# The RMS norms between the stages of a two-layer transformer trunk: squares summed by TensorE in four token parts, root and reciprocal on a quarter of the columns

## What is computed

```python
def rmsnorm(x, g):
    xf = x.astype(jnp.float32)
    y = xf * lax.rsqrt(jnp.mean(xf * xf, axis=-1, keepdims=True) + EPS)
    return (y * g.astype(jnp.float32)).astype(x.dtype)
...
def ffn_sublayer(s, m, i, g, wg, wu, wd):
    h = modulate(rmsnorm(s, g), m[3 * i], m[3 * i + 1])
    return s + 0.5 * m[3 * i + 2] * swiglu(h, wg, wu, wd)
...
    x = ffn_sublayer(x, mx, 0, p['g_ffn1'], p['w1g'], p['w1u'], p['w1d'])
    h = modulate(rmsnorm(x, p['g_mix']), mx[3], mx[4])
    u = h @ p['w_in']
    ...
    x = x + mx[5] * y
    x = ffn_sublayer(x, mx, 2, p['g_ffn2'], p['w2g'], p['w2u'], p['w2d'])
```

## Time and profile before

| | |
|---|---|
| median of 3 runs | 2639.79 us (2638.39 to 2639.95) |
| the profiled execution's own time | 2638.57 us |
| its span, first to last instruction | 2636.7 us |
| mean granted TensorE clock | 0.994 of full speed |
| TensorE matmul busy | 2554.9 us, 97% |
| VectorE, ScalarE, GpSimd busy | 2069.8, 1012.5, 163.7 us |

### The profile page before, as it was taken

One profiled execution on the slowest core, in us unless ns is written; L12 is line 12 of the kernel. 1 busy time (PEld: TensorE's weight loads), 2 busy tenths in 40 slices (PEclk: granted clock), 3 DMA queues, 4 the chain that ended last, 5 costly groups with the idle time before them and its releaser, 6 DMA issues. The chain is left out here.

```text
span 2636.7 us, 42699 instructions
## 1 busy us (share of the span) xinstructions
PE 2554.9 (97%) x15356; PEld 2363.0 (90%) x15356; DVE 2069.8 (79%) x3414; ACT 1012.5 (38%) x1854; POOL 163.7 (6%) x314
## 2 busy tenths in 40 slices
PE   6999999999997999999999899999998998999999
PEld 5899999988965889999999799999997866989998
DVE  5688888887958388888888888777768956688885
ACT  4333433333147333422332433234324256344443
POOL 2000000020003200000000200000002003100001
PEclk8999999999999999999999999999999999999999
DMA  8234323332111113333334123343232201223332
GB/s 295 64 120 136 116 92 114 124 104 64 55 57 49 33 56 105 117 93 115 123 103 136 48 90 119 98 130 119 91 104 72 88 24 47 79 83 109 99 101 79
DMA packets 192361, 253.97 MB, mean 96 GB/s; under 512 B 7278, under 2 KB 130268, under 8 KB 192220
## 3 DMA queue, kind: packets, MB, share of 16 engines
q1 hardware_dynamic: 192220, 252.07, 30.4%
HBM read 249.95 MB, written 2.10 MB: 96 GB/s over the span
## 5 line engine op out<-in xcount | busy, mean ns | idle before, releaser
L1211 PE MATMUL ps<-h_hi,w_hi 128*128 128x384 f32 (+2 forms) x2368 | 790.5, 334 | 21.9 <-DVE h_lo L2326 18.2
L1213 PE MATMUL ps<-h_hi,w_lo 128*128 128x384 f32 (+2 forms) x2368 | 785.3, 332 | 0.0
L1212 PE MATMUL ps<-h_lo,w_hi 128*128 128x384 f32 (+2 forms) x2256 | 749.3, 332 | 0.0
L1211 PEld LDWEIGHTS ps<-h_hi,w_hi 128*128 128x128 f32 x2368 | 449.3, 190 | 53.6 <-issue 22.5
L1213 PEld LDWEIGHTS ps<-h_hi,w_lo 128*128 128x128 f32 x2368 | 449.3, 190 | 20.7
L1212 PEld LDWEIGHTS ps<-h_lo,w_hi 128*128 128x128 f32 x2256 | 428.0, 190 | 19.2 <-issue 1.0
L1811 ACT ACTIVATE w_hi<-raw 128x512 fp32r<-128x512 f32 x464 | 279.7, 626 | 420.8 <-PE ps L1213 327.8
L2468 DVE TENSOR_TENSOR w_lo<-raw,w_hi 128x512 fp32r<-128x512 f32 x464 | 307.5, 684 | 14.8 <-ACT w_hi L1811 14.8
L1211 PE MATMUL ps<-t_hi_all,w_hi 128*128 128x384 f32 x864 | 292.1, 338 | 0.0
L1213 PE MATMUL ps<-t_hi_all,w_lo 128*128 128x384 f32 x864 | 292.0, 338 | 0.0
L1212 PE MATMUL ps<-t_lo_all,w_hi 128*128 128x384 f32 x864 | 291.9, 338 | 0.0
(11 more groups left out here) (276 smaller groups left out, 3994.1 us busy)
## 6 DMA issues: line engine op xcount, KB each, us to landing
side_raw<-in_w_ada SPq DMA_DIRECT2D x240, 256.0 KB, 2.7
raw<-in_w_ffn_gate SPq DMA_DIRECT2D x44, 1024.0 KB, 5.4
raw<-in_w_ffn_up SPq DMA_DIRECT2D x44, 1024.0 KB, 5.4
raw<-in_w_ffn_down SPq DMA_DIRECT2D x44, 1024.0 KB, 5.0
raw<-in_w_in SPq DMA_DIRECT2D x14, 1024.0 KB, 5.3
ada_buf<-in_w_ada SPq DMA_DIRECT2D x12, 1024.0 KB, 12.4
raw<-in_w_out SPq DMA_DIRECT2D x8, 1024.0 KB, 5.7
raw<-in_w_in SPq DMA_DIRECT2D x8, 512.0 KB, 7.2
```

Of the source, the lines that this page charges most:

```text
L1211: mm(out, wh, xh, start=start, stop=False, skip_group_check=reopened)
L1212: mm(out, wh, xl, start=False, stop=False, skip_group_check=reopened)
L1213: return mm(out, wl, xh, start=False, stop=stop, skip_group_check=reopened)
```

## The change

GpSimd's additions are gone for q = 1 to 5. Instead ScalarE writes the squares into a ring of four blocks, `sq4`, and TensorE sums them itself (`sum_squares`): each block j is four fp32 matmuls with 32 columns of ones as weights, one for each quarter of the segment's tokens, into partitions 0-31, 32-63, 64-95 and 96-127 of one bank. After the eight blocks the bank holds the sums of 64 token columns (context) or 128 (latent), a different quarter of the tokens on each group of 32 partitions. Root and reciprocal work on these 64 or 128 columns. Then TensorE spreads the result (`spread`): four fp32 matmuls with one column of the identity matrix, repeated 128 times, as weights write `rstd` of all tokens on all partitions into another bank, and VectorE's `tn` reads it from there. The plan keeps the bank of the sums out of the round from `open` to `close`, and the bank of a spread until `unblock`; the next user of the latter waits for `t_done` of the norm's last block.

The order changes with it: the sums are put between the down-projection's groups, the mixer's output groups and the blocks of the next stage's first pass; ScalarE's and VectorE's split of the second weight tile of the next stage moves behind the first root and reciprocal. The core of the diff:

```diff
+    def open(self, q, s):
+        bank = self.next_bank()
+        self.slots[("stat", q, s)] = (None, bank, self.uses[bank])
+        self.uses[bank] += 1
+        self.blocked.add(bank)
+        if bank in self.held:
+            self.spread_before[("stat", q, s)] = self.held.pop(bank)
...
+    def close(self, q, s):
+        _, bank, use = self.slots[("stat", q, s)]
+        self.slots[("stat", q, s)] = (self.n, bank, use)
+        self.n += 1
+        self.blocked.remove(bank)
...
+    def spread(self, q, s):
+        self.slot(("spread", q, s))
+        bank = self.slots[("spread", q, s)][1]
+        self.uses[bank] -= 1
+        self.blocked.add(bank)
+    def unblock(self, q, s):
+        bank = self.slots[("spread", q, s)][1]
+        self.blocked.remove(bank)
+        self.held[bank] = (q, s)
...
+        if f:
+            self.unblock((0, 2, 3, 5)[f], second)
...
+                if s == second and after < 3 * DEPTH:
+                    a_, b_ = seg_order(after)
+                    if j == 0:
+                        self.open(after, a_)
+                    if j == 1:
+                        self.close(after, a_)
+                    if j == 3:
+                        self.spread(after, a_)
+                        self.open(after, b_)
...
-        for s in (1, 0):
-            for h in range(HEADS):
-                self.slot(("K", l, h, s))
+        q = 3 * l + 1
+        keys = [("K", l, h, 1) for h in range(HEADS)]
+        for key in keys:
+            self.slot(key)
+        self.close(q, 0)
+        self.spread(q, 0)
+        self.renumber(keys)
+        self.unblock(q, 1)
+        for h in range(HEADS):
+            self.slot(("K", l, h, 0))
+            if h % 2:
+                pass
+        self.unblock(q, 0)
...
+            def sum_squares(q, s, js):
+                o, n = PIECES[s][:2]
+                bank = bank_of(("stat", q, s))
+                for j in js:
+                    if j == 0:
+                        wait_bank(pe, ("stat", q, s))
+                    pe.wait_ge(sq_done, sqcount(q, s, j))
+                    for c in range(4):
+                        at_ = n // 4 * c
+                        last = mm(ps[32 * c:32 * c + 32, bank, 0:n // 4], ones[:, 0:32], square_of(q, s, j)[:, at_:at_ + n // 4],
+                                  start=(j == 0), stop=(j == KD - 1), skip_group_check=True)
+                    if j < 4:
+                        last.then_inc(sq_summed, 1)
+                    elif j == KD - 1:
+                        last.then_inc(products, 1)
+            def spread(q, s):
+                n = PIECES[s][1] // 4
+                wait_bank(pe, ("spread", q, s))
+                pe.wait_ge(rstd_ready, rstd_number(q, s))
+                for c in range(4):
+                    last = mm(ps[:, bank_of(("spread", q, s)), n * c:n * c + n], ident[:, 32 * c:32 * c + 1].to_broadcast([128, 128]),
+                              fourths(q, s, rstd4), start=True, stop=True, skip_group_check=True)
+                last.then_inc(products, 1)
...
+                                if s == first and ws == SUM_PASS[f]:
+                                    sum_squares(q, second, sums_first(ws, k, f))
+                                    if k == SPREAD_AT[f]:
+                                        spread(q, second)
...
+                        if s == second and after < 3 * DEPTH:
+                            a_, b_ = seg_order(after)
+                            if j < 2:
+                                sum_squares(after, a_, range(4 * j, 4 * j + 4))
+                            if j == 3:
+                                spread(after, a_)
+                            if j >= 3:
+                                sum_squares(after, b_, (j - 3,))
...
+                        if s == 1 and k < 3:
+                            sum_squares(q, 0, (5 + k,))
                         if s == 1 and k == 4:
-                            stat(q, 0)
+                            spread(q, 0)
...
+                        first, second = seg_order(q + 1)
+                        if slots[0][0] == ("out", l, 4, first):
+                            sum_squares(q + 1, first, range(4))
+                            sum_squares(q + 1, second, range(4))
+                        if slots[0][0] in (("out", l, 6, first), ("out", l, 7, first)):
+                            sum_squares(q + 1, first, (slots[0][0][2] - 2,))
+                        if slots[0][0] == ("out", l, 4, second):
+                            sum_squares(q + 1, first, (6, 7))
+                        if slots[0][0] == ("out", l, 5, second):
+                            spread(q + 1, first)
+                        if slots[0][0] in (("out", l, 6, second), ("out", l, 7, second)):
+                            sum_squares(q + 1, second, (slots[0][0][2] - 2,))
...
+                if between(q):
+                    if j >= 4:
+                        act.wait_ge(sq_summed, summed_number(q, s, j - 4))
...
-                if nxt:
-                    split(nxt[1])
-                for j in range(2):
-                    square(q, second, j)
...
+                square(q, second, 0)
                 root(q, first)
+                split(nxt[1])
+                square(q, second, 1)
                 square(q, second, 2)
...
+                    if between(q) and j == 0:
+                        wait_products(dve, ("spread", q, s))
                     stt(out=tn[:, j % 2, o:o + n], in0=xT[:, j, o:o + n], scalar=amul[:, q // 3, q % 3, j, v:v + 1],
-                        in1=rstd[:, o:o + n], op0=ALU.mult, op1=ALU.mult).then_inc(t_done, 1)
+                        in1=pt(("spread", q, s), n) if between(q) else rstd[:, o:o + n], op0=ALU.mult, op1=ALU.mult)\
+                        .then_inc(t_done, 1)
...
-                    split(nxt[1])
-                    add_one(2, second)
                     last_seg = second
                     first, second = seg_order(q)
                     over_rms(q, first)
+                    add_one(2, last_seg)
+                    split(nxt[1])
```

More of the change, by code:

```diff
@@ L96, with between, sums_first @@
 SUM_NUMBER = {5: 1, 6: 2, 7: 3, 3: 4}
+def between(q):
+    return 0 < q < 3 * DEPTH
+def sums_first(w, k, f):
+    want = {"gu": {0: (5,), 1: (6,), 2: (7,)}, "g": {1: (6,), 3: (7,)}}[SUM_PASS[f]]
+    return want.get(k, ()) if w == SUM_PASS[f] else ()
 def segs_of(norm):
@@ L216, in __init__ @@
         self.bank = 0
+        self.blocked = set()
+        self.held = {}
+        self.spread_before = {}
         self.uses = [0] * 8
@@ L260, in hold, with compact @@
         self.chunk += n
+    def compact(self):
+        order = sorted((x[0], key) for key, x in self.slots.items())
+        for n, (_, key) in enumerate(order):
+            self.slots[key] = (n, *self.slots[key][1:])
     def occupants(self):
@@ L334, in side, with first_sums, renumber @@
             self.slot(("side", f, n), (self.bank + ahead) % 8)
[L336 to L341, removed]
+    def first_sums(self, f, w, k):
+        q = (0, 2, 3, 5)[f]
+        second = seg_order(q)[1]
+        if 7 in sums_first(w, k, f):
+            self.close(q, second)
+        if (w, k) == (SUM_PASS[f], SPREAD_AT[f]):
+            self.spread(q, second)
+    def renumber(self, keys):
+        for key in keys:
+            _, bank, use = self.slots[key]
+            self.slots[key] = (self.n, bank, use)
+            self.n += 1
     def ffn(self, f):
@@ L356, in ffn @@
             passes, rest = [(w, f, 0, c, s) for w in "gu" for s in (first, second) for c in range(2)], []
[L357 to L361, removed]
+        for n, key in enumerate(passes + rest):
+            if f and n == len(passes):
+                self.unblock((0, 2, 3, 5)[f], first)
+            if f == 0:
+                self.slot(key)
+                if key == ("u", 0, 0, 1, 1):
+                    self.ada(BETWEEN)
+                continue
+            group = 4 if f == 2 and n < 4 else 2
+            if n % group == 0:
+                for x in (passes + rest)[n:n + group]:
+                    self.slot(x)
+                if n == 0:
+                    for k in range(KD):
+                        self.first_sums(f, SUM_PASS[f], k)
+                    self.renumber((passes + rest)[n:n + group])
+        if f:
+            self.unblock((0, 2, 3, 5)[f], second)
         for c in range(2):
@@ L484, in mix @@
                 self.slot(("out", l, 2 * v + c, s))
-                if (v, c, s) == (2, 0, seg_order(3 * l + 2)[1]):
-                    self.slot(("stat", 3 * l + 2, seg_order(3 * l + 2)[0]))
+                first, second = seg_order(3 * l + 2)
+                if (v, c, s) == (2, 0, first):
+                    self.open(3 * l + 2, first)
+                    self.open(3 * l + 2, second)
+                if (v, c, s) == (2, 0, second):
+                    self.close(3 * l + 2, first)
+                if (v, c, s) == (2, 1, second):
+                    self.spread(3 * l + 2, first)
```

(17 more changed lines are left out.)

56 lines of the change are left out of this document (39 added, 17 removed).

## The result

The changed kernel takes 2669.43 us (median of four runs, 2669.31 to 2670.33). The kernel before takes 2639.09 (four runs, 2637.14 to 2639.95). The ratio is 1.0118, with a 95% interval of 1.0102 to 1.0134: 30 us slower. The profiled execution took 2669.39 us with a span of 2667.6, against a span of 2636.7 before, so 30.9 us are to be found in the trace.

A forecast was written before the change was run, and what follows sets the result against it. TensorE, busy for 97% of the span, bounds the kernel. Latent-pass waits 20.5 us, norm 2 4.8 and norm 5 3.0 sum to 28.3: 2638.57 becomes 2666.9, plus 1.2 for the median, 2668; range 2652 to 2682.

The forecast's parts named there:

- The latent pass: Norms 1, 3, 4: TensorE waits for a bank ScalarE frees late; 6.8, 6.9 and 6.8 us, together 20.5 slower.
- The walk up to the spread: Norm 1: TensorE's work from 569.5 to the latent spread adds up to 23.1 us; spread starts at 592.6 without waiting.
- context spread: Four full-width fp32 matmuls of 64 columns: 0.6 us, near half the 1.1 us of a latent spread of 128 columns.
- A sum alone: One block's sum between projection matmuls: 0.56 us latent, 0.45 context, of which 0.35 is the change of form.
- Norms 2 and 5: No bank wait there; TensorE's added work, less old sums and stops, makes them 4.8 and 3.0 us slower.
- Eight blocks in a row: Norm 2: eight context blocks summed in one go cost 0.45 + 3 x 0.11 + 4 x 0.21 = 1.6 us.
- The clock: Granted clock falls to 0.50 behind the new latent-pass waits; at norm 3, where it held before, 1.6 us more.
- The rule on tiling: Skill's fourfold speedup for the sums against the trace's 1.7 times; by 4 the total would be about 19 us, not 28.
- B: Rival: banks free in time; 2.6, 2.0, 2.6 us won at norms 1, 3, 4, 7.8 lost at 2 and 5: 2640; chance 0.09.
- C: Rival: new sums cost TensorE only their columns, saving about 14 us: 2626, or 2660 with the bank wait; chance 0.04.
- D: Rival: blocks in a row cost full price or more, up to 2683 or beyond; beyond its bound or slower still, chance 0.07.

The follow-up runs named there:

- experiment 1: Changed kernel with another PSUM bank for one tile of each latent pass at norms 1, 3 and 4: 2642.22 us, ratio to before 1.0016.
- experiment 2: Kernel before, given only the changed kernel's pattern of banks at norms 1, 3 and 4, no new matmuls: 2675.14 us, ratio 1.0143.
- experiment 3: New sums and spreads only at norms 2 and 5, norms 1, 3 and 4 as in the kernel before: 2644.82 us, ratio 1.0032.
- experiment 5: On top of experiment 1, the same sums drawn together in pairs or fours, 17 stretches less: 2635.55 us, ratio to before 0.9995.
- experiment 7: Experiment 1 with one full matmul per block instead of four parts, no spreads, its bank edits left out: 2655.39 us, ratio to before 1.0065.
- the best version: New sums only at norms 1, 3 and 4, with experiment 1's mended bank and latent sums in pairs: 2630.40 us, ratio to before 0.9975.

## Why the prediction was right

It said 2668 in a range of 2652 to 2682, and 2669.4 came. (The range is a little off its own bounds, 2654 to 2683, which decides nothing here.) The mechanism was right; some of the closeness is luck, since errors of several tenths cancelled in the walk and at norm 5. By its own steps:

**The latent pass (20.5 us of 28.3).** Right in the mechanism, shown from both sides: experiment 1 takes the wait away and gets 25 to 27 us back, experiment 2 makes it in a kernel without the change and loses 37.9. The profile did not name the releaser in the changed kernel ("issue"), though it does so in experiment 2; only the bank plan told of it beforehand. The pass was forecast for 607.2 and started at 606.90; at norm 3 for a shift of 5.3 and came at 5.4 (19.3 behind, less 13.9).

The Trainium skill, Perfetto Trace Analysis, section Matmuls, says that independent matmul groups should rotate through different PSUM banks, so that one group's evacuation overlaps the next group's matmuls. These traces agree, with a number for what one tile out of the rotation costs: 7.2 to 7.5 us of waiting in the changed kernel and 12.8 in experiment 2.

**The walk up to the spread.** The forecast was 592.6; it started at 592.58. To the hundredth that is luck: the context spread in the walk cost 0.3 us more than forecast, and the changed kernel was 0.3 ahead when the walk began (first row of the table). VectorE was done in time, with its reciprocal ended at 591.10, and `tn` out of PSUM took 0.75 us as before. A sum alone was put at 0.56, and this is what it costs (timeline of TensorE in the changed kernel):

```profile
578.91 0.39 PE L1341 MATMUL ps<-even_hi_all,w_lo 128*128 128x512 f32 x1
579.23 0.43 PE L1374 MATMUL ps<-sq,ones 128*32 128x128 f32 x8
579.59 0.50 PE L1339 MATMUL ps<-even_hi_all,w_hi 128*128 128x512 f32 x1
579.93 0.39 PE L1340 MATMUL ps<-even_lo_all,w_hi 128*128 128x512 f32 x1
```

579.93 - 578.91 - 2 x 0.23 = 0.56. But the spreads cost 0.9 each whatever their width: 593.59 - 592.46 - 2 x 0.12 = 0.89 for 128 columns, forecast 1.1, and for 64 columns the same, forecast 0.6:

```profile
939.60 0.39 PE L1341 MATMUL ps<-h_hi,w_lo 128*128 128x512 f32 x1
939.83 1.00 PE L1387 MATMUL ps<-rstd,ident 128*128 128x64 f32 x8
940.64 0.48 PE L1339 MATMUL ps<-h_hi,w_hi 128*128 128x512 f32 x1
940.95 0.39 PE L1340 MATMUL ps<-h_lo,w_hi 128*128 128x512 f32 x1
```

940.95 - 939.60 - 2 x 0.23 = 0.89. This is the step that was mis-sized: "since the columns halve" does not hold for a full-width fp32 matmul of 64 columns here. At norm 5 both spreads have 64 columns, so it adds 0.6 us there. A second term was missing altogether, a stop for the last square:

```profile
2306.83 0.32 PE L1374 MATMUL ps<-sq,ones 128*32 128x64 f32 x8 [0.75 <-ACT sq L2001]
```

Against these 1.3 us stands 0.7 that the forecast did not take off. Most of it, 0.5, is at a wait of the kernel before for the low part of a weight, at 2303.22, which the changed kernel does not have; the rest is at the two old sums and the stop of 1.8, which together made up 2.9 and not 2.7. So 3.6 came for 3.0, by errors that partly cancel.

**Norms 2 and 5 (7.8 us).** 7.6 in experiment 3 by the times, 8.5 in the traces. At norm 2 the two spreads were off in opposite directions, 0.3 dearer and 0.2 cheaper. Eight blocks in a row, forecast 1.6, cost 919.01 - 917.12 - 2 x 0.12 = 1.65:

```profile
917.12 0.28 PE L1341 MATMUL ps<-h_hi,w_lo 128*128 128x256 f32 x1
917.33 1.53 PE L1374 MATMUL ps<-sq,ones 128*32 128x64 f32 x64
...
919.01 0.28 PE L1340 MATMUL ps<-h_lo,w_hi 128*128 128x256 f32 x1
```

**The clock.** Right in its place behind the waits, too dear at norm 3, and missing elsewhere. After the waits the granted clock is at 0.50, at norm 3 too, where it had held before (stretches of TensorE in the changed kernel: length, busy, granted clock):

```profile
1503.00:1506.00 3.00, 0.33 (x1) 0.50 0.00 0
1507.00:1510.00 3.00, 3.00 (x11) 0.72 0.00 0
```

At norm 3 it cost 0.9 us net (19.3 to 20.2 behind), where 1.6 had been forecast. What the forecast missed is a fall far from any norm, in the first mixer's attention. The same view of the kernel before:

```profile
753.00:756.00 3.00, 3.00 (x20) 0.91 0.00 0
756.00:759.00 3.00, 3.00 (x6) 0.53 0.00 0
759.00:762.00 3.00, 3.00 (x10) 1.00 0.00 0
```

and of the changed kernel, the same work some 7 us later:

```profile
759.00:762.00 3.00, 3.00 (x27) 0.86 0.00 0
762.00:765.00 3.00, 3.00 (x10) 0.50 0.00 0
765.00:768.00 3.00, 3.00 (x4) 0.50 0.00 0
768.00:771.00 3.00, 3.00 (x10) 1.00 0.00 0
```

It stays down about twice as long, and there lie 1.6 of the 2.2 us of the table that belong to no norm. The other 0.6 is a stop that the kernel before does not have, eleven microseconds ahead of it:

```profile
749.91 1.56 PE L1867 MATMUL ps<-kT,qT 64*128 64x384 f32 x8 [0.52 <-issue]
```

The two are most of the difference between the sum (28.3) and the spans (30.9). That the change lengthened the fall is not shown, since executions of one program differ in their falls (last section), and the cause of the stop is open.

**The rule on tiling.** The Trainium skill, TensorEngine Tiling (Array Packing), section Overview, gives up to 4x where a dimension is at most 32, and its Tiling Modes says that a change of mode drains the engine. Experiments 5 and 7 measured both sides: 0.86 to 0.56 is 1.5 times for a block alone, and what a change back and forth takes is 0.34, so the second block of a pair, 0.22, is 3.9 times cheaper than a full one. The factor of the page is there, and the change of form eats most of it when each block stands alone.

**The rivals.** B (banks free in time, 2640) is what experiment 1 built: 2642.2, and by its trace 2.7, 2.4 and 2.6 us won at norms 1, 3 and 4 against 8.4 lost at norms 2 and 5, where 2.6, 2.0, 2.6 and 7.8 had been worked out. C falls with experiments 3 and 5. D stayed outside: blocks in a row were cheap, and a spread cost 0.9 us, under the 1.1 forecast for 128 columns and over the 0.6 for 64. What sets this price, the loading of the weights or something else, is not shown.

## What to carry to other kernels

When a change takes tiles out of a round of PSUM banks, print for every tile its bank and who held it last, in time as well as in order: most of the loss here was not in the added instructions but in one tile per norm whose bank had been filled seven to eight microseconds earlier and was freed only behind a whole norm. Then price an added matmul by where it stands, not by its columns: here a narrow one among wide ones cost 0.34 us for the change of form, so draw them together. And take such a change only where it covers a wait (norms 1, 3 and 4 here); elsewhere leave the idle engine its work.

## What the runs showed of the hardware

A full-width fp32 matmul with 64 columns costs as much as one with 128: 0.89 us for a spread of four in either width. The eight recorded instructions start 0.11 us apart in both.

The same program runs with more or fewer falls of the clock. The profiled execution of experiment 1 had a mean clock of 0.997 and took 2637.59 us; eight of its eleven runs had 0.994 or 0.995 and took 2641.5 to 2643.0. The other three, the profiled one among them, had 0.997 and took 2637.5 to 2637.6. So some 5 us of this kernel go with the clock, as much as the whole gain of the best version, and a change of 0.2% needs its runs' clocks beside it.

The profile can fail to name a wait for a bank. The same wait on the same ScalarE copy is "issue" in the changed kernel and `kT` in experiment 2. What gave it away was that TensorE started 0.1 us after a copy ended.
